# A hybrid decoder layer on one core: the experts' second weights are reloaded by ScalarE instead of SyncE

## What is computed

```python
def moe_ffn(h, w_router, b_router, w1, b1, w2, b2):
    ...
    top_vals, top_idx = lax.top_k(logits, TOP_K)
    gates = jax.nn.softmax(top_vals, axis=-1)
    ...
    def expert_block(args):
        tok, e = args
        xb = x_pad[tok]
        gu = xb @ w1[e] + b1[e]
        gate = jnp.minimum(gu[:, :F], SWIGLU_LIMIT)
        up = jnp.clip(gu[:, F:], -SWIGLU_LIMIT, SWIGLU_LIMIT)
        act = (up + 1.0) * gate * jax.nn.sigmoid(SWIGLU_ALPHA * gate)
        return act @ w2[e] + b2[e]
    ...
```

## Time and profile before

| | |
|---|---|
| Time, median of 3 runs | 1331.26 us (1330.33 to 1332.33) |
| The profiled execution's own time | 1331.19 us |
| Its span, first to last instruction | 1329.4 us |
| Mean granted clock of TensorE | 0.98 of full speed |
| TensorE busy | 1187.6 us, 89% of the span |
| ScalarE busy | 245.3 us, 18% |
| HBM read | 460.89 MB |
| Loads in the expert loop | 192 of 2048 KB, median 24.3 us from issue to landing |

### The profile page before, as it was taken

How to read it: one execution, slowest core, us unless ns; L and a number is a source line. 1 busy time by engine, 2 the same in 40 slices (tenths; PEclk the granted TensorE clock), 3 DMA queues, 4 the chain that set the end, 5 groups by cost and what they waited for, 6 DMA issues and landing times.

```text
span 1329.4 us, 17731 instructions
## 1 busy us (share of the span) xinstructions
PE 1187.6 (89%) x7407; PEld 631.8 (48%) x7407; DVE 375.4 (28%) x678; ACT 245.3 (18%) x313; POOL 40.0 (3%) x41
## 2 busy tenths in 40 slices
PE   6999999999649999898999888989998899999985
PEld 5999887998523333333333333333333333333332
DVE  4434654523661221112112111211211112112112
ACT  4444543431400100001100000110000001100001
POOL 0000000000550000000000000000000000000000
PEclk9999999999769999999999999999999999999998
DMA  8745533942519999999999999999999999999993
GB/s 293 242 142 182 184 127 139 368 158 92 201 52 431 428 427 429 429 427 429 430 427 429 430 427 429 429 428 429 429 428 429 429 428 428 429 428 428 430 427 160
DMA packets 55459, 462.33 MB, mean 348 GB/s; under 512 B 6577, under 2 KB 6634, under 8 KB 30858
## 3 DMA queue, kind: packets, MB, share of 16 engines
q1 hardware_dynamic: 51768, 457.46, 82.8%
q0 software_dynamic: 864, 2.77, 0.6%
q10 hardware_dynamic: 2802, 1.74, 0.4%
HBM read 460.89 MB, written 1.07 MB: 348 GB/s over the span
## 4 chain that ended last, share of the span: by engine, by line
DMA 54%; PE 40%; POOL 3%; issue 1%; ACT 1%; DVE 1%; SPq 0%; DVEq 0%; ACTq 0%; POOLq 0%
DMA w_ring<-in_w 51%; PE ps L865 13%; PE ps L680 4%; PE ps L682 3%; PE ps L683 3%; PE ps L894 3%; PE ps L810 2%; PE ps L687 2%; PE ps L689 2%; PE ps L688 2%; DMA attT<-in_b 2%; PE ps L805 1%; POOL attT L453 1%; DMA w_ring<-in_w_in 1%; PE ps L913 1%
## 5 line engine op out<-in xcount | busy, mean ns | idle before, releaser
L865 PE MATMUL ps<-w_ring,A_W 128*64 128x512 f32 x2048 | 465.4, 598 | 61.6 <-DMA w_ring<-in_w 61.6
L865 PEld LDWEIGHTS ps<-w_ring,A_W 128*64 128x64 f32 x2048 | 139.7, 137 | 347.0 <-issue 232.8
L894 PE MATMUL ps<-w_ring,A_W 128*64 128x512 f32 x1024 | 225.9, 592 | 0.0
L610 ACT ACTIVATE A_W<-A_W 128x512 f32<-128x512 f32 x32 | 20.2, 630 | 779.9 <-DVE A_W L1239 779.9
L1239 DVE TENSOR_SCALAR A_W<-ps 128x512 f32<-128x512 f32 x32 | 22.1, 692 | 483.4 <-PE ps L865 483.4
L894 PEld LDWEIGHTS ps<-w_ring,A_W 128*64 128x64 f32 x1024 | 85.1, 137 | 119.3 <-issue 117.7
L965 DVE TENSOR_TENSOR w_parts<-w_ring,w_parts 128x1024 fp32r<-128x1024 f32 x76 | 92.5, 1224 | 109.8 <-ACT w_parts L493 105.9
L680 PE MATMUL ps<-hT_hi,w_parts 128*128 128x256 f32 x384 | 110.2, 287 | 2.0 <-ACT hT_hi L512 2.0
L682 PE MATMUL ps<-hT_lo,w_parts 128*128 128x256 f32 x384 | 109.3, 285 | 0.0
L683 PE MATMUL ps<-hT_hi,w_parts 128*128 128x256 f32 x384 | 109.2, 284 | 0.0
L493 ACT ACTIVATE w_parts<-w_ring 128x1024 fp32r<-128x1024 f32 x76 | 79.9, 1056 | 86.5 <-PE ps L683 54.6
(11 more groups left out here) (198 smaller groups left out, 845.6 us busy)
## 6 DMA issues: line engine op xcount, KB each, us to landing
w_ring<-in_w SPq DMA_DIRECT2D x192, 2048.0 KB, 24.3
w_ring<-in_w_in SPq DMA_DIRECT2D x38, 1024.0 KB, 7.1
w_ring<-in_w_ret_branch SPq DMA_DIRECT2D x2, 2048.0 KB, 12.2
A_W<-in_w_out SPq DMA_DIRECT2D x1, 2560.0 KB, 13.1
xb<-in_x SPq DMA_DIRECT2D x4, 512.0 KB, 3.8
A_QK<-in_w_att_branch SPq DMA_DIRECT2D x1, 2048.0 KB, 9.8
w_ring<-bias_scratch POOLq DMA_DIRECT2D x1, 1536.0 KB, 11.3
A_W<-in_w_out SPq DMA_DIRECT2D x1, 1536.0 KB, 7.5
```

Source lines behind the costliest of these rows:

```text
L865: mm = pe.matmul(o, XT[:, k, :], w1_ring[:, k, c * HALF:(c + 1) * HALF], start=(k == 0), stop=(k == KC - 1))
L894: mm = pe.matmul(ps[CAP * c:CAP * c + CAP, 7, :], lhs, w2_ring[:, q, c * HALF:(c + 1) * HALF], start=False, stop=(q == FQ - 1))
```

## The change

The reloads of w2 (experts 1 to 31) leave SyncE's loop and are issued by ScalarE, behind its last copy of a round and with the same waits. ScalarE's loop is one round shorter, and its last round is written out behind it, without reloads. The first w2 loads (expert 0) and those of the extra loop stay with SyncE.

```diff
@@ -401,9 +401,6 @@
                 for u in range(W1_UNITS):
                     sp.wait_ge(main.w1_used, e * W1_UNITS - (W1_UNITS - 1 - u))
                     load_w1(sp, main, e, u)
-                for u in range(W2_UNITS):
-                    sp.wait_ge(main.w2_used, e * W2_UNITS - (W2_UNITS - 1 - u))
-                    load_w2(sp, main, e, u)
 
             sp.wait_ge(main.w1_used, N_EXP * W1_UNITS)
             sp.wait_ge(main.w2_used, N_EXP * W2_UNITS)
@@ -613,11 +610,20 @@
+            def reload_w2(e):
+                for u in range(W2_UNITS):
+                    act.wait_ge(main.w2_used, e * W2_UNITS - (W2_UNITS - 1 - u))
+                    load_w2(act, main, e, u)
+
             store_x(main, 0)
-            with act.Fori(0, N_EXP) as i:
+            with act.Fori(0, N_EXP - 1) as i:
                 sigmoid(main, i)
                 store_x(main, i + 1)
                 store_act_low(main, i)
+                reload_w2(i + 1)
+            sigmoid(main, N_EXP - 1)
+            store_x(main, N_EXP)
+            store_act_low(main, N_EXP - 1)
```

## The result

| | time, median us (lowest to highest) | ratio to before, 95% interval |
|---|---|---|
| before | 1330.8 (1329.75 to 1332.33) | |
| after | 1337.77 (1337.24 to 1340.76) | 1.0056 [1.0038, 1.0074] |

The change makes the kernel slower by 7.0 us from median to median, where +6.7 and 1337.9 had been predicted. The ratio is not the quotient of the two medians, which would be 1.0052; the two ways of comparing differ by half a microsecond here. Among the executions of the kernel before that stand beside the exchanged queues, "all but the last expert" and the smaller loads, one took 2486.44 us; it is left out, and the median of the six others is 1331.5. The profiled execution took 1337.24 us, 6.05 more than that of before, with a span of 1335.3.

What follows compares the result with a forecast made beforehand. DMA bounds the expert loop at 29.36 us a round; the last w1 load landing 6.2 to 7.2 us later, middle +6.7, on the profiled 1331.19 gives 1337.9 us, range 1331.0 to 1343.

Steps and rivals of the forecast that it cites:

- What sets the pace: Expert loop: DMA at 428 GB/s keeps rounds at 29.36 us and data ending at 1306; issuing from ScalarE costs 0.
- Sharing by halves: Loop DMA: q1 and q10 served one record in turn, both of 16 KB, so each gets half the bytes; 60%.
- (b): Rival on DMA order: q10 is served first, nothing of w2 stays behind the last w1 load; +9.8 us, 1341.0; 5%.
- (c): Rival: w2 loads wait for q1's backlog as now, its records being fetched ahead; not slower, 1331.2; 13%.
- (a): Rival on DMA turns: whole loads alternate, one w2 load stays behind the last w1 load; +4.9 us, 1336.1; 10%.
- The last w1 load lands late and the work behind it follows: End of the loop: last w1 load lands 6.2 to 7.2 us later, 31.2 us of work follow; +6.7 us.
- The steady state: Loop rounds: recurrence settles within five rounds at 29.36 us each, with one TensorE wait of 2.4 us per round.
- R: What is left of the next expert's four w1 loads when w2's bytes join, in us of DMA; 7.2, corrected 6.2.
- The correction for the late start of q10: A queue starting against a backlog starts some 2.0 us late: 15.0 becomes 17.0, R 6.2; the middle, +6.7 us, taken.
- (e): Rival: TensorE's single 2.4 us wait halves its clock; large case loop 31 us longer, 1369, 2%; otherwise under 1 us.
- (d): Rival: two streams move fewer bytes, 5.9 us per 1% of rate lost over 588 us; 1344 and up; 7%.
- (f): Rival: two queues fill gaps of one; 1% more rate gives back 5.9 us, faster needs over 1.6%; 3%.

Runs made afterwards that it cites:

- exchanged queues: Against the kernel before, ScalarE issues the w1 reloads ahead of its sigmoid and SyncE the w2 reloads: 1336.68 us against 1331.5, ratio 1.0047.
- all but the last expert: The changed kernel, but SyncE issues the last expert's two w2 reloads, behind the last w1 load: 1337.12 us against 1331.5 of the kernel before, ratio 1.0051.
- smaller loads: w1 in eight loads of 1024 KB instead of four of 2048 KB: in the kernel before 1337.76 us, in the changed kernel 1347.1, against 1331.5.
- only the last expert moved: Against the kernel before, only the last expert's two w2 reloads are issued by ScalarE: 1341.07 us against 1331.33, ratio 1.0075.
- three experts moved: Against the kernel before, only the w2 reloads of experts 29, 30 and 31 are issued by ScalarE: 1338.47 us, ratio 1.0050.

## Why the prediction was right, and where it was not

**What sets the pace: right.** The DMA rate did not change (428), the end of the data did not (1306), and issuing from ScalarE costs nothing (all loads there: 0.9998). ScalarE's wait ahead of the sigmoid is still up to 21.5 us long:

```profile
ACT A_W L607 <- DVE A_W L1245: 465.0, 29, 21.5
```

**Sharing by halves: right.** The window of 1291 to 1299 us of the kernel after:

```profile
DMA packets 225, 3.42 MB, mean 428 GB/s; under 512 B 16, under 2 KB 16, under 8 KB 16
...
q1 hardware_dynamic: 121, 1.72, 50.6%
q10 hardware_dynamic: 104, 1.70, 49.9%
```

1.72 MB against 1.70. Rivals (b), q10 first, and (c), q1's records already committed, are excluded by it; (c) also by the start of q10 3.2 to 4.2 us after its issue where the backlog was 14 us. Whole loads in turn, (a), could look even over 8 us, since a load takes 4.9; the single microseconds with only the last expert moved exclude it, 15 records to 15.

**The last w1 load lands late and the work behind it follows: right.** +5.97 in the profiled execution, with 31.1 us behind it, just under the +6.2 to +7.2 predicted; the median moved by 7.0. Undoing the sharing in the last four rounds alone removes all of it.

**The steady state: wrong.** I let the recurrence settle on R = 7.2 and on one wait of 2.4 us in each round of 29.36, and said that it gets there within five rounds. The rounds really take 26.6 to 34.7 us, and the waits reach 5.0. Two things had been left out. The remainder of w2, 9.79 - R, stands in the way of the next expert's w1: of the 15.0 us before the next w2 joins, w1 gets 15.0 - (9.79 - R), and of its 19.57 us this leaves R' = 14.36 - R. A deviation from 7.2 changes its sign from round to round and is not damped. The exchanged queues show just that at full clock: rounds of 28.75 and 30.0 us, by 15.0 + 2R an R of 6.9 and 7.5, which add up to 14.4. The second thing is the clock: behind the long stop of the kernel after, the next quarter took 2.9 us more (6.50 against 3.65). That this is what widens the swing there to 34.7 us is argued and not shown; no run holds the clock fixed.

So the loss is not a fixed 7.2 but depends on where in this cycle the loop ends: the variants measured +5.2 to +9.7. That my value was met to 0.3 us is in good part luck. (The executions of the changed kernel lie 3.5 us apart, but those of the kernel before, which has no such cycle, lie as much as 3.7 apart, so that spread says nothing of it.)

Two more readings were off. I put TensorE's need at 27.0 us by taking the two waits off a round of 29.36; rounds without a stop take 26.6. The quarters overlap a little: three on end take 10.47 us together, less than three times 3.60 to 3.65. And I expected w1 loads of the third and fourth place to take longer to land; in the last round of the kernel after the fourth took 24.27 us where it had taken 25.39, and all w1 loads in the loop have a median of 18.8, for a TensorE that is late also asks later.

The correction for the late start of q10 was 2.0 us, by half of its size in R. No run isolates what it did to the time, but the rows bear out its size: in the kernel before, the first reload, issued at 394.00 with the engines idle, has its first records between 395 and 396, 1 to 2 us later; against the backlog it was 3.2 to 4.2.

**The clock (e): half right.** It falls behind most of the long stops; the kernel as a whole pays little for it, since the weights go on landing meanwhile. I had given only the large case a chance, and the small one, which came, "under 1 us". In the run with three experts moved it cost 1.7 us in the last quarter.

**The rate (d) and the gain (f):** neither came. The kernel with two queues for 27 rounds is not measurably slower or faster than with one, so 27 rounds of sharing cost about 1 us in all at most (the interval's end).

The Trainium skill (DMA: Bandwidth & Descriptors, Issuing engines are not separate DMA queues) says that spreading loads over issuing engines saves only issue time. For bandwidth these runs agree, 428 either way. Taken as a rule on the kernel's time, as in rival (c), it fails here: the second queue changed the order of arrival, and that was worth 0.56%.

No version here beats the kernel before by more than a measurement can tell.

## What to carry to other kernels

In a loop bound by DMA, one queue in the order of use is a schedule: it lets the loads that are needed last arrive last, behind work that covers them. A second issuing engine gave up that order here without giving bandwidth, and its price was a lateness that appears once, at the end, and not per round. Look at what hangs behind the last load, and test by moving only the last round. A recurrence that one works out for such a loop should be tried with a disturbance before its fixed point is believed.

## What the runs showed of the hardware that I had not expected

- Two queues share an engine by record and not by byte: 70 to 72 records with 16 KB and 8 KB, 1.15 to 0.51 MB.
- With w1 in loads of 1024 KB and records of 8 KB the loop's mean rate was 424 GB/s instead of 428, enough to turn a gain of 4 us into a loss of 6.
- TensorE's clock fell after shorter stops than I had thought: the quarters behind stops of 2.29 us (three experts moved) and 3.30 (one moved) took 5.35 us instead of 3.65, and behind the stop of 5.03 us in the kernel after the clock was 0.52 over 6 us; with stops of 1.1 and 1.24 us in every round it stayed at full speed. The length of the stop is not all: with the queues exchanged, stops of 2.79 and 3.81 us left the quarter at 3.65.
- TensorE was 7.3 us behind in the round of expert 26 and made it up by that of expert 30 once the loads went back to one queue, although the DMA had no idle time to lend: the weights landed early while TensorE was late, and a round without a stop takes it 26.6 us where the loads take 29.36.
